# Forget-gate attention: one transpose for two heads, decay rows loaded beside the turned heads, six fillers at the opening

## The chip, the core and the metric

The kernel runs on one core of a Trainium2 chip. The metric is the device time of one execution in microseconds (us). The core has a matrix engine (TensorE, PE in the rows), VectorE (DVE), ScalarE (ACT), GpSimd (POOL) and SyncE (SP), each with its own instruction queue that is worked off in order; they wait for one another through semaphores. Matrix products are written to PSUM and have to be copied to SBUF by DVE or ACT. DMAs are issued from the queues of SP, ACT and POOL.

## What is computed

Two transformer blocks in float32, over 256 positions of width 1024, one after the other. The change touches the first attention of the first block, and in it the forget-gate heads ("fox"); around it stand gated feed-forward parts (ffn), a differential attention and, in the second block, two further mixers.

```python
def causal_block_attention(q, k, v, log_decay_cum=None):
    scale = q.shape[-1] ** -0.5
    for i in range(seq // Q_BLOCK):                     # blocks of 128 queries
        q0, q1 = i * Q_BLOCK, (i + 1) * Q_BLOCK
        s = einsum('bhqd,bhkd->bhqk', q[:, :, q0:q1], k[:, :, :q1]) * scale
        if log_decay_cum is not None:
            s = s + log_decay_cum[:, :, q0:q1, None] - log_decay_cum[:, :, None, :q1]
        ...                                             # causal mask, softmax, times v

def token_mixer(h, w_in, fox_forget_b, ...):
    fq, fk, fv, fgate, dq, dk, dv = split(h @ w_in)     # 8 fox heads of 64, 4 differential heads
    log_f = log_sigmoid(fgate + fox_forget_b)
    c = cumsum(log_f, axis=1)                           # one row of 256 sums for each fox head
    fox_o = causal_block_attention(fq, fk, fv, c)
    ...                                                 # differential attention, then @ w_out
```

The sums c enter the scores of a fox head as two further rows: the queries carry (c, 1) and the keys (1, -c) beside their 64 features, so one product of 66 rows gives q.k + c[t] - c[s].

## The kernel before

**Weights.** Every weight matrix comes in pieces of 128 x 2048. SP loads a piece into one of three slots (raw), ACT rounds it (hi, line 1207), DVE takes the rest (lo, line 1779), and PE multiplies the two parts in three products (lines 582, 585, 586). PE waits for a piece's lo. All engines' queues are written out by hand, step by step, so the order of the code is the order of the work.

**The projection (w_in).** Its blocks of 512 columns are copied out of PSUM by ACT for the first 128 positions and by DVE for the second (evac, line 1957 on DVE) into the large tile proj. Blocks 0 to 2 are the differential q, k, v, blocks 3 and 4 the fox q and k, block 5 the fox v. Half blocks are numbered h = 0 to 23; after each, ACT and DVE do the copy-out that is due and the next piece's hi or lo (after, next_lo). Meanwhile DVE works out log f (line 2243), clears qd_sb (line 2245, its tile is called att_dec in the rows), and PE forms the sums c with three small products (lines 1078 to 1080) behind h = 8. PE goes on to the attention when the decay columns are written (aug_ready).

**POOL's rotation.** When blocks 0 and 1 are copied out (evac_a and evac_d at 2), POOL rotates parts of the differential q and k, 12 operations (lines 1723 to 1728), and raises roped. PE waits for roped before it turns pair 0.

**The attention (diff_and_fox).** It goes by pairs p: 0 to 3 are the four differential heads, 4 to 7 the fox heads two by two. For each pair PE turns q and k by transposes (turn_qk, line 854) into the PSUM bank turned; ACT copies q out (q_out), DVE copies k out (k_out); PE forms scores (lines 872 to 877; the products with id16 and mask16 add the causal mask), DVE finds maxima, ACT takes exp, PE turns the weights (line 884) and multiplies with v (lines 896 to 898), DVE scales the result (line 2052 for fox heads). Products of projections that are still due (behind, products) stand between these steps. For the fox pairs each head's 64 columns and 2 decay columns lie together in proj (AUG = 66 columns a head), so a head is turned by itself: 8 transposes of 66 columns a pair, with both tiles of positions and q and k. The turned heads go to q_sb and k_sb (att_q and att_k in the rows), 66 rows each. The scores of pair 5 wait besides for DVE's scaling of two pieces of the turned differential output (fill_scaled, line 1797; turn_scaled).

**The opening.** Until the first weights are there, PE multiplies zeros (warm_up, line 646): 7 fillers, the first four transposes of x, 3 fillers, then the first product (line 667), which waits for ACT's first rounded part.

Of the kernel before, what the change touches and what calls it, by code (L numbers as in the profile page):

```python
# [11 lines left out]
ALU = mybir.AluOpType  # L12
# [27 lines left out]
FQ, FK, FV, DQ, DK, DV, MIX = 0, 8 * AUG, 16 * AUG, 16 * AUG + 512, 16 * AUG + 1024, 16 * AUG + 1536, 16 * AUG + 2048  # L40
# [80 lines left out]
def build(nc, x_d, wg_d, wu_d, wd_d, win_d, wout_d, win2_d, whg_d, wat_d, wout2_d,  # L121
          fixed_d, rows_d, post_d, rel_d, level_d, hot_d, out_d, row_d, skew_d):

    with ExitStack() as ctx:
# [80 lines left out]
        def heads(ap, n):  # L205
# [28 lines left out]
        log_f_ready, decay_sum, aug_ready, padded = (  # L234
            sem("log_f_ready"), sem("decay_sum"), sem("aug_ready"), sem("padded"))
# [103 lines left out]
        def win_place(b, t):  # L339

            if b < 3:
                return proj[:, t, DQ + b * BLK:DQ + (b + 1) * BLK]
            if b < 5:
                return heads(proj[:, t, (b - 3) * 8 * AUG:(b - 2) * 8 * AUG], 8)[:, :, 0:64]
            return proj[:, t, FV:FV + BLK]

# [232 lines left out]
        def _(pe):  # L579
# [68 lines left out]
            def first_block():  # L648
# [28 lines left out]
                warm_up(3)  # L677
# [165 lines left out]
            def turn_qk(p):  # L843

                kind, i = pair(p)
                for n in range(2):
                    for h in range(1 if kind == 1 else 2):
                        for t in range(TT):
                            if kind == 0:
                                src = proj[:, t, ((FQ, FK)[n] + (2 * i + h) * AUG):((FQ, FK)[n] + (2 * i + h + 1) * AUG)]  # L850
                            else:
                                col = (DQ, DK)[n] + i * P if kind == 1 else (AQ, AK)[n] + i * S + h * P
                                src = proj[:, t, col:col + P]
                            mm = pe.transpose(turned[0:src.shape[1], n, h * S + t * P:h * S + (t + 1) * P], src, idn)  # L854
                mm.then_inc(qkT_full, 1)

            def scores(p):
                kind = pair(p)[0]
                pe.wait_ge(qT_ready, p + 1)
                pe.wait_ge(kT_ready, p + 1)  # L860
                if p in (1, 2, 3, 9, 10, 11):
# [5 lines left out]
                rows_used = AUG if kind == 0 else P  # L867
                for h in range(2):
                    q = (qd_sb if kind == 1 else q_sb)[0:rows_used, h, :]
                    k = k_sb[0:rows_used, 0 if kind == 1 else h, :]  # L870
# [328 lines left out]
        def _(act):  # L1199
# [151 lines left out]
            def q_out(p):  # L1351
                kind = pair(p)[0]
# [1209 lines left out]
```

## Time and profile before

| | |
|---|---|
| time, median of 3 runs | 1019.68 us (1019.23 to 1020.27) |
| the profiled execution | 1020.19 us |
| its span, first to last instruction | 1018.4 us |
| PE busy | 1012.3 us, 99% |
| DVE busy | 713.0 us, 70% |
| ACT busy | 486.9 us, 48% |
| POOL busy | 201.5 us, 20% |
| TensorE's granted clock, mean of the span | 1.00 |

The time is what a run takes on the device; the span is what the profile sees, from the first to the last instruction. Busy times are shares of the span. PE's busy time counts pipelined matmuls whose ends are modelled, so a stretch of PE is best read by the starts of its instructions. A timeline row gives start, duration, engine, line, operation, what it writes and reads, how many instructions are merged, and in brackets the idle time before it with what ended it.

### The profile page before, as it was taken

How to read it: one execution, taken by the hardware profiler on the slowest of the kernel's cores; microseconds unless marked ns; L12 is line 12 of the kernel's file. 1: busy time of each engine (PE TensorE's matmuls, PEld its weight loads, DVE VectorE, ACT ScalarE, POOL GpSimd, SP SyncE). 2: the span in 40 equal slices, each digit the busy share in tenths (PEclk: the TensorE clock that was granted, in tenths of full speed). 3: DMA queues.
4: the chain of work that ended last, by engine and by line, in shares of the span. 5: the costliest groups of instructions: out<-in, count | busy, mean ns of one | idle time of the engine just before them, and what ended most of it. 6: DMA issues, size and time to landing. Idle time of an engine off the chain costs nothing.

```text
span 1018.4 us, 14449 instructions
## 1 busy us (share of the span) xinstructions
PE 1012.3 (99%) x5240; PEld 856.1 (84%) x5240; DVE 713.0 (70%) x821; ACT 486.9 (48%) x606; POOL 201.5 (20%) x198
## 2 busy tenths in 40 slices
PE   8999999999999999999999999999999999999998
PEld 6888888888888888888888888888888888888887
DVE  6766666765678767676764589986877677666664
ACT  6544344554555544444544454545446354434342
POOL 2313131121100223222110070033000002313130
PEclk9999999999999999999999999999999999999999
DMA  9664556664324556565746554444435645555551
GB/s 317 213 206 165 206 169 222 227 189 128 119 84 166 166 170 206 182 208 182 244 149 196 178 166 138 146 128 161 136 102 182 204 167 206 165 206 170 201 197 51
DMA packets 116809, 178.62 MB, mean 175 GB/s; under 512 B 5656, under 2 KB 73760, under 8 KB 116640
## 3 DMA queue, kind: packets, MB, share of 16 engines
q1 hardware_dynamic: 115952, 174.82, 51.4%
q0 software_dynamic: 512, 1.55, 0.6%
q10 hardware_dynamic: 304, 1.70, 0.5%
q8 instruction: 27, 0.44, 0.2%
q14 instruction: 14, 0.11, 0.0%
HBM read 176.98 MB, written 2.63 MB: 176 GB/s over the span
## 4 chain that ended last, share of the span: by engine, by line
PE 99%; DMA 0%; ACT 0%; issue 0%; SPq 0%; DVE 0%
PE acc L582 11%; PE acc L586 11%; PE acc L585 11%; PE tp L762 10%; PE gu L762 10%; PE gu L765 5%; PE tp L765 5%; PE tp L582 4%; PE tp L586 4%; PE tp L585 4%; PE gu L582 4%; PE gu L586 4%; PE gu L585 4%; PE acc L1002 2%; PE gu L872 1%; PE acc L854 1%
## 5 line engine op out<-in xcount | busy, mean ns | idle before, releaser
L1779 DVE TENSOR_TENSOR wlo<-raw,whi 128x2048 fp32r<-128x2048 f32 x149 | 349.1, 2346 | 157.2 <-ACT whi L1207 156.4
L1207 ACT ACTIVATE whi<-raw 128x2048 fp32r<-128x2048 f32 x150 | 285.8, 1908 | 61.8 <-PE acc L586 26.7
L762 PE MATMUL tp<-act_in,whi 128*128 128x512 f32 x432 | 103.0, 391 | 0.0
L762 PE MATMUL gu<-act_in,whi 128*128 128x512 f32 x432 | 102.6, 390 | 0.0
L1700 POOL TENSOR_TENSOR sil<-sil,tmp 128x256 f32<-128x256 f32 x54 | 88.9, 1646 | 33.6 <-ACT sil L1279 33.6
L1698 POOL TENSOR_TENSOR tmp<-tmp 128x256 f32<-128x256 f32 x54 | 39.8, 737 | 281.5 <-DVE tmp L1898 281.5
L762 PEld LDWEIGHTS gu<-act_in,whi 128*128 128x128 f32 x432 | 80.9, 188 | 16.6
L582 PE MATMUL acc<-whi,hT_hi 128*128 128x512 f32 x240 | 94.0, 392 | 0.0
L585 PE MATMUL acc<-wlo,hT_hi 128*128 128x512 f32 x240 | 93.7, 390 | 0.0
L586 PE MATMUL acc<-whi,hT_lo 128*128 128x512 f32 x240 | 93.4, 389 | 0.0
L762 PEld LDWEIGHTS tp<-act_in,whi 128*128 128x128 f32 x432 | 79.7, 188 | 16.1 <-issue 0.4
L1284 ACT ACTIVATE hT_hi<-hid 128x256 fp32r<-128x256 f32 x54 | 22.2, 417 | 138.5 <-DVE hid L1909 129.6
L582 PE MATMUL tp<-whi,act_in 128*128 128x512 f32 x192 | 77.4, 403 | 0.0
L586 PE MATMUL tp<-whi,act_in 128*128 128x512 f32 x192 | 75.0, 391 | 0.0
L585 PE MATMUL tp<-wlo,act_in 128*128 128x512 f32 x192 | 74.8, 390 | 0.0
L582 PE MATMUL acc<-whi,act_in 128*128 128x512 f32 x176 | 70.9, 403 | 0.0
L1279 ACT ACTIVATE sil<-tmp 128x256 f32<-128x256 f32 x54 | 22.1, 409 | 100.3 <-POOL tmp L1698 100.3
L586 PE MATMUL acc<-whi,act_in 128*128 128x512 f32 x176 | 68.7, 391 | 0.0
L585 PE MATMUL acc<-wlo,act_in 128*128 128x512 f32 x176 | 68.6, 390 | 0.0
L1681 POOL TENSOR_SCALAR ms<-sums 128x1 f32<-128x1 f32 (+2 forms) x20 | 11.3, 566 | 268.9 <-ACT junk L1229 159.7
L765 PEld LDWEIGHTS gu<-act_in,wlo 128*128 128x128 f32 x432 | 55.4, 191 | 2.1
L765 PEld LDWEIGHTS tp<-act_in,wlo 128*128 128x128 f32 x432 | 55.4, 191 | 2.1
(327 smaller groups left out, 1830.5 us busy)
## 6 DMA issues: line engine op xcount, KB each, us to landing
raw<-in_w_in SPq DMA_DIRECT2D x96, 512.0 KB, 4.5
raw<-in_down SPq DMA_DIRECT2D x66, 512.0 KB, 4.0
raw<-in_gate SPq DMA_DIRECT2D x64, 512.0 KB, 4.1
raw<-in_up SPq DMA_DIRECT2D x64, 512.0 KB, 4.7
raw<-in_w_out SPq DMA_DIRECT2D x16, 512.0 KB, 4.6
raw<-in_w_branch_hg SPq DMA_DIRECT2D x8, 512.0 KB, 4.6
raw<-in_w_branch_attn SPq DMA_DIRECT2D x8, 512.0 KB, 4.7
post<-in_post_gains SPq DMA_DIRECT2D x3, 512.0 KB, 6.7
```

What stands on the lines that cost most here:

```text
L582: pe.matmul(out, hi, w_hi, start=start, stop=False)
L585: pe.matmul(out, hi, w_lo, start=False, stop=False)
L586: return pe.matmul(out, lo, w_hi, start=False, stop=stop)
L762: pe.matmul(banks[:, a, :], w_hi[:, i, a * P:(a + 1) * P], both, start=i == 0, stop=False)
L765: mm = pe.matmul(banks[:, a, 0:S], w_lo[:, i, a * P:(a + 1) * P], act_in[:, i, 0, :], start=False, stop=i == KT - 1)
L1002: mm = pe.matmul(acc[:, hh, i // 2, i % 2 * 256:i % 2 * 256 + QN], k_at(t, h), hg_queries(t)[:, h, :], start=True, stop=True)
L1207: act.activation(split_weights(k)[0], raw[:, k % RING, :], ACT.Copy).then_inc(hi_ready, 1)
L1279: act.activation(sil[:, a, :], gate[:, a, :], ACT.Silu).then_inc(sil_ready, 1)
L1284: act.activation(hT_hi[:, a, :], hid[:, a, :], ACT.Copy).then_inc(hT_hi_ready, 1)
L1698: pool.tensor_tensor(gate[:, a, :], gate[:, a, :], row, ALU.mult).then_inc(gate_scaled, 1)
L1700: pool.tensor_tensor(sil[:, a, :], sil[:, a, :], row, ALU.mult).then_inc(sil_scaled, 1)
L1779: dve.tensor_tensor(w_lo, raw[:, k % RING, :], w_hi.bitcast(F32), ALU.subtract).then_inc(lo_ready, 1)
```

## The change

1. The fox q and k of all heads lie in proj without gaps (FQ, FK at multiples of 512), and two heads are turned by one transpose of 128 columns: 4 transposes a pair instead of 8.
2. The turned heads no longer go to q_sb and k_sb. Each head has a place of its own in a free part of proj (fox_q in the first tile of positions, fox_k in the second). Of a pair, the first head takes rows 0 to 63, the second rows 64 to 127, since that is where the transpose puts them. ACT and DVE so write two pieces of 64 x 256 where they wrote one of 66 x 512.
3. The decay rows lie beside them: rows 64 and 65 for a first head, rows 0 and 1 for a second, whose rows 2 to 63 are zero. The scores use 66 rows for a first head and 128 for a second. DVE clears and sets these rows with six memsets of 1024 elements in a partition, ahead of the memset of qd_sb.
4. The sums c are formed as rows (8 x 256 instead of 128 x 16), copied by DVE to a scratch tile, stored to DRAM by POOL, and loaded by POOL with four small DMAs. POOL does this behind its rotation and ahead of the norms of the differential heads. The scores of pair 4 wait for the loads (aug_in).
5. The opening has 6 fillers ahead of the first product instead of 3.

```diff
-FQ, FK, FV, DQ, DK, DV, MIX = 0, 8 * AUG, 16 * AUG, 16 * AUG + 512, 16 * AUG + 1024, 16 * AUG + 1536, 16 * AUG + 2048
+FQ, FK, FV, DQ, DK, DV, MIX = (512 * n for n in range(7))
+FOX_AT = 5120
...
+        fox_q, fox_k = (heads(proj[:, t, FOX_AT:FOX_AT + 8 * S], 8) for t in range(TT))
+        decay_rows = xs[0:8, 1, 0:S]
...
-                warm_up(3)
+                warm_up(6)
...
                 for n in range(2):
-                    for h in range(1 if kind == 1 else 2):
+                    for h in range(2 if kind == 2 else 1):
                         for t in range(TT):
-                            if kind == 0:
-                                src = proj[:, t, ((FQ, FK)[n] + (2 * i + h) * AUG):((FQ, FK)[n] + (2 * i + h + 1) * AUG)]
...
-                            mm = pe.transpose(turned[0:src.shape[1], n, h * S + t * P:h * S + (t + 1) * P], src, idn)
+                            col = ((FQ, FK)[n] + i * P, (DQ, DK)[n] + i * P, (AQ, AK)[n] + i * S + h * P)[kind]
+                            mm = pe.transpose(turned[:, n, h * S + t * P:h * S + (t + 1) * P], proj[:, t, col:col + P], idn)
...
+                if p == 4:
+                    pe.wait_ge(aug_in, 16 * 4)
...
-                rows_used = AUG if kind == 0 else P
                 for h in range(2):
+                    rows_used = AUG if kind == 0 and h == 0 else P
+                    if kind == 0:
+                        q, k = (a[0:rows_used, 2 * i + h, :] for a in (fox_q, fox_k))
...
-            pe.matmul(tp[:, 1, 0:8], tri, f[0], start=True, stop=True)
-            pe.matmul(tp[:, 1, 8:16], ones, f[0], start=True, stop=False)
-            pe.matmul(tp[:, 1, 8:16], tri, f[1], start=False, stop=True).then_inc(decay_sum, 1)
+            pe.matmul(tp[0:8, 1, 0:P], f[0], tri, start=True, stop=True)
+            pe.matmul(tp[0:8, 1, P:S], f[0], ones, start=True, stop=False)
+            pe.matmul(tp[0:8, 1, P:S], f[1], tri, start=False, stop=True).then_inc(decay_sum, 1)
...
+                elif kind == 0:
+                    act.activation(fox_q[0:64, 2 * i, :], turned[0:64, 0, 0:S], ACT.Copy, scale=FOX_SCALE)
+                    act.activation(fox_q[64:P, 2 * i + 1, :], turned[64:P, 0, 0:S], ACT.Copy, scale=FOX_SCALE)\
+                       .then_inc(qT_ready, 1)
...
             pool.nop().then_inc(roped, 1)
+            pool.wait_ge(aug_ready, 1)
+            pool.wait_ge(rows_spread, 16)
+            pool.dma_start(bass.AP(tensor=row_d.tensor, offset=0, ap=[[S, 8], [1, S]]), decay_rows).then_inc(aug_out, 16)
+            pool.wait_ge(aug_out, 16)
+            for a, r in ((fox_q, 0), (fox_k, 1)):
+                for h, at in ((0, 64), (1, 0)):
+                    dst = a.rearrange("p (i two) n -> p i two n", two=2)[at + r:at + r + 1, :, h, :]
+                    pool.dma_start(dst, bass.AP(tensor=row_d.tensor, offset=h * S, ap=[[8 * S, 1], [2 * S, 4], [1, S]]))                        .then_inc(aug_in, 16)
             norm("diff")
...
-                    dve.tensor_copy(k_sb[0:AUG, :, :], heads(turned[0:AUG, 1, :], 2)).then_inc(kT_ready, 1)
+                    dve.tensor_copy(fox_k[0:64, 2 * i, :], turned[0:64, 1, 0:S])
+                    dve.tensor_copy(fox_k[64:P, 2 * i + 1, :], turned[64:P, 1, 0:S]).then_inc(kT_ready, 1)
...
+            for a, one in ((fox_q, -1.0), (fox_k, 1.0)):
+                of_pairs = a.rearrange("p (i two) n -> p i two n", two=2)
+                link(dve.memset(of_pairs[0:64, :, 1, :], 0.0))
+                dve.memset(of_pairs[0:2, :, 1, :], one)
+                dve.memset(of_pairs[64:66, :, 0, :], one)
             dve.memset(qd_sb, 0.0).then_inc(padded, 1)
...
-                    dve.wait_ge(evac_a, 2)
-                    c = tp[:, 1, 0:16].rearrange("p (t h) -> p t h", t=TT)
...
-                    dve.tensor_scalar(q2[:, :, :, 64], c, 8.0, None, ALU.mult)
-                    dve.tensor_scalar(k2[:, :, :, 65], c, -1.0, None, ALU.mult)
-                    dve.memset(q2[:, :, :, 65], 8.0)
-                    dve.memset(k2[:, :, :, 64], 1.0).then_inc(aug_ready, 1)
+                    dve.tensor_copy(decay_rows, tp[0:8, 1, 0:S]).then_inc(aug_ready, 1)
```

On DVE, from the log of the gates (lf) to the decay columns, this stood in a row before (att_dec is qd_sb, wlo the rest of a weight piece, proj<-acc a copy-out of the projection):

```order
L2243 SCALAR_TENSOR_TENSOR lf<-lf 128x16
L2245 MEMSET att_dec 128x512
L1779 TENSOR_TENSOR wlo<-raw,whi 128x2048
L1957 TENSOR_SCALAR proj<-acc,rstd 128x512
L1779 TENSOR_TENSOR wlo<-raw,whi 128x2048 x2
L2255 TENSOR_SCALAR proj<-tp 128x2x8
L2256 TENSOR_SCALAR proj<-tp 128x2x8
L2257 MEMSET proj 128x2x8
L2258 MEMSET proj 128x2x8
```

and this stands there now:

```order
L2259 SCALAR_TENSOR_TENSOR lf<-lf 128x16
L2263 MEMSET proj 64x4x256
L2264 MEMSET proj 2x4x256
L2265 MEMSET proj 2x4x256
L2263 MEMSET proj 64x4x256
L2264 MEMSET proj 2x4x256
L2265 MEMSET proj 2x4x256
L2266 MEMSET att_dec 128x512
L1794 TENSOR_TENSOR wlo<-raw,whi 128x2048
L1972 TENSOR_SCALAR proj<-acc,rstd 128x512
L1794 TENSOR_TENSOR wlo<-raw,whi 128x2048 x2
L2273 COPY xs<-tp 8x256
```

Six memsets have come in ahead of the first weight rest and of the copy-out of block 1, which POOL's rotation waits for; the four small operations behind the rests have become one copy.

On POOL, from the end of the rotation to the first norm of the differential heads, this stands now (before, the last line of the rotation was followed by the norm at once):

```order
L1732 TENSOR_TENSOR xs<-proj,fixed 128x128
L1733 TENSOR_TENSOR xs<-proj,fixed 128x128
L1734 TENSOR_TENSOR proj<-xs 128x16x8
L1735 TENSOR_TENSOR proj<-xs 128x16x8
L1739 DMA bias_rows<-xs 8x256
L1744 DMA proj<-bias_rows 1x4x256 x4
L1688 TENSOR_SCALAR ms<-sums 128x2
```

The five DMAs stand between the rotation and the norm.

On PE, the scores of pair 4 and the turn of pair 5 behind them, before (id and mask add the causal mask):

```order
L872 MATMUL tp<-att_k,att_q 128x256
L874 MATMUL tp<-mask,id 128x128
L875 MATMUL tp<-att_k,att_q 128x128
L877 MATMUL tp<-mask,id 128x128
L872 MATMUL tp<-att_k,att_q 128x256
L874 MATMUL tp<-mask,id 128x128
L875 MATMUL tp<-att_k,att_q 128x128
L877 MATMUL tp<-mask,id 128x128
L854 MATMUL acc<-fixed,proj 66x128 x8
```

and now:

```order
L876 MATMUL tp<-proj 128x256
L878 MATMUL tp<-mask,id 128x128
L879 MATMUL tp<-proj 128x128
L881 MATMUL tp<-mask,id 128x128
L876 MATMUL tp<-proj 128x256
L878 MATMUL tp<-mask,id 128x128
L879 MATMUL tp<-proj 128x128
L881 MATMUL tp<-mask,id 128x128
L854 MATMUL acc<-fixed,proj 128x128 x4
```

The order is the same; the turn has 4 transposes for 8, and the scores read the heads' own places.

## Rows read from the trace of the kernel before

**Rows 1.** The page, part 1: busy us (share of the span) xinstructions of each engine.

```profile
PE 1012.3 (99%) x5240; PEld 856.1 (84%) x5240; DVE 713.0 (70%) x821; ACT 486.9 (48%) x606; POOL 201.5 (20%) x198
```

**Rows 2.** The page, part 4: the chain that ended last, by engine.

```profile
PE 99%; DMA 0%; ACT 0%; issue 0%; SPq 0%; DVE 0%
```

**Rows 3.** Timeline of PE, opening: start us, us, engine line op out<-in xcount [idle before <-releaser].

```profile
5.03 0.81 PE L646 MATMUL gu<-junk 128*128 128x512 bf16 x3
...
7.35 0.47 PE L667 MATMUL gu<-whi,act_in 128*128 128x512 f32 x1 [1.51 <-ACT whi L1469]
```

**Rows 4.** Stretches of PE, opening: stretch, us, PE busy (x), granted clock, DMA, GB/s.

```profile
6.00:7.00 1.00, 0.00 (x0) 1.00 1.07 372
```

**Rows 5.** Timeline of DVE, projection, 217 to 231 us.

```profile
217.34 0.48 DVE L2245 MEMSET att_dec<- 128x512 f32 x1
220.43 2.29 DVE L1779 TENSOR_TENSOR wlo<-raw,whi 128x2048 fp32r<-128x2048 f32 x1 [2.61 <-ACT whi L1207]
222.64 0.74 DVE L1957 TENSOR_SCALAR proj<-acc,rstd 128x512 f32<-128x512 f32 x1
223.30 2.28 DVE L1779 TENSOR_TENSOR wlo<-raw,whi 128x2048 fp32r<-128x2048 f32 x1
228.15 2.55 DVE L1779 TENSOR_TENSOR wlo<-raw,whi 128x2048 fp32r<-128x2048 f32 x1 [2.56 <-ACT whi L1207]
```

**Rows 6.** Groups by form, DVE: line, operation, shapes, xcount | busy us, mean ns | idle.

```profile
L1982 DVE COPY att_k<-acc 66x512 f32<-66x512 f32 x4 | 2.7, 685 | 2.4 <-PE acc L854 2.4
L1980 DVE COPY att_k<-acc 128x256 f32<-128x256 f32 x4 | 1.7, 425 | 6.0 <-PE acc L854 6.0
...
L2258 DVE MEMSET proj<- 128x16 f32 x1 | 0.1, 72 | 0.0
```

**Rows 7.** Timeline of PE, projection: decay products, piece 5's first product, pair 0's turn.

```profile
222.52 0.28 PE L1078 MATMUL tp<-lf,fixed 128*128 128x8 f32 x2
...
223.11 0.48 PE L582 MATMUL acc<-whi,act_in 128*128 128x512 f32 x1
...
225.94 0.39 PE L582 MATMUL acc<-whi,act_in 128*128 128x512 f32 x1
...
234.10 0.60 PE L854 MATMUL acc<-fixed,proj 128*128 128x128 f32 x4
```

**Rows 8.** Timeline of POOL: the rotation's blocked operations, its last, the first norm.

```profile
223.56 2.33 POOL L1723 TENSOR_TENSOR xs<-proj,fixed 128x128 f32<-128x128 f32 x1 [17.83 <-DVE proj L1957]
...
228.51 2.48 POOL L1724 TENSOR_TENSOR xs<-proj,fixed 128x128 f32<-128x128 f32 x1
...
232.29 0.46 POOL L1728 TENSOR_TENSOR proj<-xs 128x128 f32<-128x128 f32 x1
256.39 0.19 POOL L1681 TENSOR_SCALAR ms<-sums 128x2 f32<-128x2 f32 x1 [23.64 <-ACT junk L1393]
```

**Rows 9.** Groups by form, PE: scores of 128 and of 66 rows, 128 columns.

```profile
L875 PE MATMUL gu<-att_k,att_dec 128*128 128x128 f32 x16 | 3.5, 302 | 0.0
...
L875 PE MATMUL gu<-att_k,att_q 66*128 66x128 f32 x8 | 1.7, 301 | 0.0
```

**Rows 10.** DMA issues: out<-in queue op xcount, KB each, median us to landing.

```profile
rel<-in_rel_table POOLq DMA_DIRECT2D x1, 1.0 KB, 4.6
```

**Rows 11.** Timeline of PE, attention: turns of pairs 2 and 4 and what follows.

```profile
253.84 0.60 PE L854 MATMUL acc<-fixed,proj 128*128 128x128 f32 x4
254.27 0.39 PE L896 MATMUL gu<-proj,att_pT 128*128 128x128 f32 x2
...
275.19 1.03 PE L854 MATMUL acc<-fixed,proj 128*66 128x128 f32 x8
276.06 0.39 PE L896 MATMUL gu<-proj,att_pT 128*128 128x128 f32 x2
```

**Rows 12.** Timeline of PE, attention: the first product of pair 5's scores.

```profile
286.43 0.67 PE L872 MATMUL gu<-att_k,att_q 66*128 66x256 f32 x2
```

**Rows 13.** Timeline of DVE, attention: the scaling that pair 5's scores wait for.

```profile
285.01 1.28 DVE L1797 TENSOR_TENSOR tmp<-gu,fixed 128x512 f32<-128x512 f32 x2
```

More of the change, by code:

```diff
@@ L233, in build @@
         gate_product, gate_abs, gate_log = sem("gate_product"), sem("gate_abs"), sem("gate_log")
-        log_f_ready, decay_sum, aug_ready, padded = (
-            sem("log_f_ready"), sem("decay_sum"), sem("aug_ready"), sem("padded"))
+        log_f_ready, decay_sum, aug_ready, aug_out, aug_in, padded = (
+            sem("log_f_ready"), sem("decay_sum"), sem("aug_ready"), sem("aug_out"), sem("aug_in"), sem("padded"))
         lb_in, lb_exp, lam_in, lam_exp = sem("lb_in"), sem("lb_exp"), sem("lam_in"), sem("lam_exp")
@@ L343, in win_place @@
             if b < 5:
-                return heads(proj[:, t, (b - 3) * 8 * AUG:(b - 2) * 8 * AUG], 8)[:, :, 0:64]
+                return proj[:, t, (b - 3) * BLK:(b - 2) * BLK]
             return proj[:, t, FV:FV + BLK]
+        fox_q, fox_k = (heads(proj[:, t, FOX_AT:FOX_AT + 8 * S], 8) for t in range(TT))
+        decay_rows = xs[0:8, 1, 0:S]
         def fill_bank(u, i):
@@ L846, in turn_qk @@
                 for n in range(2):
[L847 removed]
+                    for h in range(2 if kind == 2 else 1):
                         for t in range(TT):
[L849 to L854 removed]
+                            col = ((FQ, FK)[n] + i * P, (DQ, DK)[n] + i * P, (AQ, AK)[n] + i * S + h * P)[kind]
+                            mm = pe.transpose(turned[:, n, h * S + t * P:h * S + (t + 1) * P], proj[:, t, col:col + P], idn)
                 mm.then_inc(qkT_full, 1)
             def scores(p):
[L858 removed]
+                kind, i = pair(p)
                 pe.wait_ge(qT_ready, p + 1)
                 pe.wait_ge(kT_ready, p + 1)
+                if p == 4:
+                    pe.wait_ge(aug_in, 16 * 4)
                 if p in (1, 2, 3, 9, 10, 11):
@@ L866, in scores @@
                     pe.wait_ge(turn_scaled, scaled_n(turn_n(T_WOUT) + 1))
-                rows_used = AUG if kind == 0 else P
                 for h in range(2):
-                    q = (qd_sb if kind == 1 else q_sb)[0:rows_used, h, :]
-                    k = k_sb[0:rows_used, 0 if kind == 1 else h, :]
+                    rows_used = AUG if kind == 0 and h == 0 else P
+                    if kind == 0:
+                        q, k = (a[0:rows_used, 2 * i + h, :] for a in (fox_q, fox_k))
+                    else:
+                        q, k = (qd_sb if kind == 1 else q_sb)[:, h, :], k_sb[:, 0 if kind == 1 else h, :]
                     lt, el = late(p)[:, h * S:(h + 1) * S], early(p)[:, h * P:(h + 1) * P]
@@ L1351, in q_out @@
             def q_out(p):
-                kind = pair(p)[0]
+                kind, i = pair(p)
                 act.wait_ge(qkT_full, p + 1)
@@ L1357, in q_out @@
                     act.activation(qd_sb[64:P, 1, :], turned[64:P, 0, 0:S], ACT.Copy, scale=FOX_SCALE).then_inc(qT_ready, 1)
-                else:
-                    r = AUG if kind == 0 else P
-                    act.activation(q_sb[0:r, :, :], heads(turned[0:r, 0, :], 2), ACT.Copy,
-                                   scale=FOX_SCALE if kind == 0 else cols[:, G_QG:G_QG + 1]).then_inc(qT_ready, 1)
+                elif kind == 0:
+                    act.activation(fox_q[0:64, 2 * i, :], turned[0:64, 0, 0:S], ACT.Copy, scale=FOX_SCALE)
+                    act.activation(fox_q[64:P, 2 * i + 1, :], turned[64:P, 0, 0:S], ACT.Copy, scale=FOX_SCALE)\
+                       .then_inc(qT_ready, 1)
+                else:
+                    act.activation(q_sb[:, :, :], heads(turned[:, 0, :], 2), ACT.Copy,
+                                   scale=cols[:, G_QG:G_QG + 1]).then_inc(qT_ready, 1)
             def exps(p):
@@ L1976, in k_out @@
             def k_out(p):
-                kind = pair(p)[0]
+                kind, i = pair(p)
                 dve.wait_ge(qkT_full, p + 1)
```

1 line of the change is left out of this document (removed).

## The prediction

> **What bounds the kernel now.** I read the busy times first [rows 1]: TensorE (PE) is busy 1012.3 of 1018.4 us, so only some 6 us of the span are not matmul. The chain of waits says the same [rows 2]: 99% of the chain that ended last is PE. So an edit counts only if it takes time out of PE's own row, or makes PE wait where it does not wait now. DVE, ACT, POOL and the DMAs matter only at the points where PE waits for them, and each has to be looked at in its own place. I then went through the timelines in three places: the opening, the stretch from 217 to 235 us in which the first projection ends and the attention begins, and the attention of pairs 4 to 7 (the forget-gate pairs) from 275 us on.
>
> **The opening: three more fillers, nothing.** The three fillers ahead of the first product take 0.81 us together, and PE then stands for 1.51 us until ACT has split the first weights [rows 3]. Three more, at the same 0.27 us, end at about 6.65 us; the first product starts at 7.35 us. That idle time hides them, with 0.7 us over; if it were gone they would cost at most 0.8 us. Can they gain? Only if the idle time cost PE its clock. The granted clock is 1.00, its upper level of 2.4 GHz, in the very microsecond in which PE does nothing [rows 4], so there is nothing to win back. I take 0, with ends of -0.3 and +0.8 us.
>
> **The projection stage: six memsets on DVE.** They stand right behind the log of the gates, ahead of the memset of qd_sb (before: at 217.34 us). Each writes 1024 elements in a partition. The trace has no memset that long; it has 512 elements at 0.48 us [rows 5] and 16 at 72 ns [rows 6], a slope of 0.83 ns an element, so 0.91 us for 1024, and with the small overlap of neighbours about 0.87 us from start to start. Two of them are followed by a wait of DVE for itself; I allow 0.1 us each, small beside the bounds. Sum: 6 x 0.87 + 0.2 = 5.4 us. The other bound is the rate of DVE's copies, 425 ns for 256 and 685 ns for 512 elements [rows 6], 1.02 ns an element: 1.2 us for 1024, 7.0 us in all. The lower bound is what the short memsets give if two partitions cost less than 128, which no row shows. I take 5.4, since that is the slope of the same operation.
> By the Trainium skill, "VectorE: DVE Perf Modes", section "Zero memsets can be issued as uint32 (trn2)", a memset takes one cycle an element; with the 0.96 GHz of its page "Trainium Kernel Development and Optimization", section "NeuronCore Architecture", that is an estimate of 1.07 us each and 6.6 us in all, so 1.2 us more wait at the end of the sum below; the trace's 512 elements in 0.48 us are less than the 0.53 us that this gives, so I stay with the row.
>
> Behind the memsets DVE's queue holds: the rest of a weight piece (lo of piece 5 of w_in), the copy-out of block 1, the rests of pieces 6 and 7, then the decay. Before, DVE had 2.61 us of idle time ahead of the first of these, which started at 220.43 us [rows 5]. Now the memsets end at 217.34 + 5.4 = 222.75, qd_sb at 223.2, and piece 5 starts 2.8 us late, at 223.2, and ends at 225.5. PE takes piece 5 at 225.94 us [rows 7]. So this wait stays covered, by 0.4 us. The copy-out, before at 222.64, comes at 225.4 and ends at 226.2; piece 6 runs from 226.1 to 228.4, piece 7 from 228.3 to 230.9.
>
> **The same delay on POOL, and there it is not covered.** POOL's rotation (12 operations, lines 1723 to 1728) waits for that copy-out. Before, it began at 223.56 and ended at 232.29 + 0.46 = 232.75 [rows 8], and PE, which waits for it before it turns pair 0, came to that turn at 234.10 [rows 7]: 1.35 us of cover, less about 0.2 us for the signal (0.14 us at the place in rows 12 and 13, and a nop ahead of it). Two of the twelve operations took 2.33 and 2.48 us where the others take 0.44: each began while DVE ran a weight rest, and ended 0.3 us after it (225.89 against 225.58, 230.99 against 230.70) [rows 5, 8]. So a rest on DVE holds POOL up for its whole length. Now POOL begins at 226.35. Its first operation ends 0.3 us after piece 6, at 228.7; the second is held by piece 7 and ends at 231.2; the other ten at 0.44 us (the last four before took 1.76 us) end at 235.65. With 0.2 us for the signal PE turns pair 0 at 235.85 instead of 234.10: **+1.75 us**. PE has nothing to put there, since its queue is in order, and everything behind shifts by as much. If the first operation too is held until piece 7 is done, the end is 235.8; the bounds come from the memsets: 7.0 instead of 5.4 us puts it to +3.35 us.
>
> **The decay itself.** The three products become 128 columns wide with 8 columns of weights; each is two records. Before they took 222.52 to 223.11, 0.59 us [rows 7]. The nearest rows with 128 columns show a busy share of 3.5/16 = 0.22 us a record [rows 9], so at most 1.3 us; the lower bound is the 0.59 us of now. Since the turn of pair 0 now starts when POOL is done, up to 1.5 us more ahead of it costs nothing; without that wait I would add 0.1 to 0.7 us. DVE's four small operations become one copy of 256 elements (0.4 us); PE's wait for it (aug_ready) comes at about 231.4, and DVE is there at 231.3; a miss of a few tenths would hide in the same wait.
>
> **The rows by way of DRAM.** POOL issues one store, waits for it, then four loads. All of it stands behind the rotation and ahead of the norms of the differential heads. POOL's small loads land after 4.6 us [rows 10]. Even at 2 us for each issue, more than I expect, the store is in by 242.3, the loads are issued by 250.3 and in by 255. The first norm is wanted at 256.39, after POOL has stood for 23.64 us [rows 8], and it needs only the issues. The new wait for the rows stands before the scores of pair 4, at 278.8 us (now 1.75 later): cover of some 25 us. Cost 0. Queues SP and ACT are not touched.
>
> **Pairs 4 to 7: the turns.** Four transposes of 128 columns take 253.84 to 254.27 = 0.43 us; eight of 66 take 275.19 to 276.06 = 0.87 us [rows 11]. A transpose costs PE the same at 66 or 128 columns, so half as many save 0.44 us a pair, 1.76 us in four. The scores are not dearer: the 66-row and the 128-row form take 301 and 302 ns [rows 9]. On ACT and DVE one copy of 66 x 512 becomes two of 64 x 256: DVE 685 ns becomes about 0.76 us [rows 6], 0.08 us more, where the next step waits for DVE.
> Not all four pairs can keep it. Pair 4: PE goes on into products that are ready; 0.44 saved. Pair 5: after its turn PE comes to the scores of pair 5, which start at 286.43 [rows 12], 0.14 us after DVE has scaled two pieces of the output turn (285.01 + 1.28 = 286.29) [rows 13]. DVE's queue up to there starts from the scores of pair 4, ahead of the turn, so it gets no earlier; the 0.44 us turn into a wait, and DVE's 0.08 us come on top: -0.08 saved. Pairs 6 and 7: DVE's queue starts from the turn itself, so it moves with it; 0.44 less up to 0.08, 0.40 each. Sum: 0.44 - 0.08 + 0.40 + 0.40 = **1.16 us saved**. Ends: 1.76 (no wait takes it) and 0.36 (only pair 4 keeps it, pair 5 as above).
>
> **The sum.** +1.75 - 1.16 + 0 = +0.6 us. The profiled execution took 1020.19 us, of which 1018.4 are span and 1.8 lie around it; it would take 1020.8. The median of the runs shown is 0.5 us lower, 1019.68: I forecast **1020.3 us**. A measurement of this kernel can tell about 0.2%, 2.04 us, from no change; so this is no change.
>
> **Rivals.**
> *The rotation is not late* (the memsets are short, or the first rests leave POOL room). It decides from a delay of 1.05 us of DVE, that is memsets of 3.7 us in all, 0.57 us each. Against it: the slope of the memset rows. For it: four of the six write two partitions only. Then the turns' 1.16 us stay, less 0.1 to 0.7 for the decay: 1018.7 us, and 1017.9 if all four pairs keep theirs. Chance 0.18.
> *The memsets run at the rate of copies*, the slow side, at the one place PE meets POOL's rotation: +3.35 - 1.16 = +2.2, 1021.9 us. Slower by more than 0.2% from memsets of 1.15 us on. On its way piece 5 is late for PE too (226.7 and later against 225.94), which does not add, since PE's later wait takes it in. For it: the copies' slope, and the longest memset seen is half as long. Against: the two memset rows. Chance 0.15.
> *The turns save nothing*, each pair ending in a wait as pair 5 does: +1.75 + 0.3 = +2.1, 1021.8 us. For it: what the rows show at pair 5. Against: pairs 4, 6 and 7 have their DVE work behind the turn. Chance 0.05.
> Anything else, such as the loads landing late: 0.04.
>
> **Chances and range.** The forecast (1019.7 to 1020.9) has 0.58. Faster by over 0.2% (under 1017.64) takes the low end of the first rival and something unseen: 0.06. Slower (over 1021.72): half of the second and third and the tail, 0.16. Within: 0.78. The range, 1018.3 to 1022.0, takes in most of both first rivals and leaves out under 2 in 10.
>
> **What would show it.** Each memset at 0.9 us, and piece 5's rest starting near 223.2 us; POOL's rotation ending near 235.7; PE standing 1.5 to 1.8 us before the turn of pair 0, with POOL named; four transposes in 0.43 us at pairs 4 to 7, and a wait of some 0.5 us before the scores of pair 5, for DVE; the loads landed by 255 us; the first product at 7.35 us as now. I am wrong if PE does not stand before the turn of pair 0, if the scores of pair 4 wait for a DMA, or if the opening moves.

## The result, and the profile after

| | before | after |
|---|---|---|
| median of the runs made together (11 each) | 1019.53 us | 1022.13 us (1021.74 to 1022.32) |
| the profiled execution | 1020.19 us | 1021.74 us |
| its span | 1018.4 us | 1019.9 us |

The ratio is 1.0024, with a 95% interval of 1.0015 to 1.0034. The kernel became slower by 2.6 us. That is just past the 0.2% (2.04 us) which the prediction set as its bound, and the interval reaches to both sides of that bound. The forecast, 1020.3 us, is 1.8 us too low, and 1022.13 lies 0.13 us above the upper end of the range.

The page of after, parts 1 and 4 (busy us, share of the span and instructions of each engine; the chain of waits by engine), answers to [rows 1, 2]:

```profile
PE 1012.3 (99%) x5227; PEld 854.0 (84%) x5227; DVE 718.6 (70%) x828; ACT 487.4 (48%) x610; POOL 203.9 (20%) x203
...
PE 96%; DVE 2%; POOL 1%; issue 1%; ACT 0%; POOLq 0%
```

PE is busy for as long as before, 1012.3 us, and the span is 1.5 us longer. So the loss is waiting, and the chain now has shares of DVE and POOL that it did not have. The waits of PE between 195 and 330 us of after (engine, line, what it waited for: us in total, times, longest) name the places; the kernel before shows none there:

```profile
PE acc L854 <- POOLq L1736: 1.4, 1, 1.4
PE acc L586 <- DVE wlo L1794: 0.7, 1, 0.7
PE gu L876 <- DVE tmp L1812: 0.5, 1, 0.5
PE tp L876 <- DVE proj L2068: 0.3, 1, 0.3
```

The first two are the delay of DVE at piece 5 and of POOL at the turn of pair 0; the last two stand before the scores of pairs 5 and 6. The timeline of DVE in after, projection (start us, us, engine line operation; in brackets the idle time before and what ended it), answers to [rows 5]:

```profile
216.51 0.91 DVE L2263 MEMSET proj<- 64x1024 f32 x1 [0.15 <-issue]
217.69 0.91 DVE L2264 MEMSET proj<- 2x1024 f32 x1 [0.27 <-DVE proj L2263]
218.85 0.91 DVE L2265 MEMSET proj<- 2x1024 f32 x1 [0.25 <-issue]
220.01 0.91 DVE L2263 MEMSET proj<- 64x1024 f32 x1 [0.25 <-issue]
221.19 0.91 DVE L2264 MEMSET proj<- 2x1024 f32 x1 [0.27 <-DVE proj L2263]
222.35 0.91 DVE L2265 MEMSET proj<- 2x1024 f32 x1 [0.25 <-issue]
223.42 0.48 DVE L2266 MEMSET att_dec<- 128x512 f32 x1 [0.15 <-issue]
223.82 2.23 DVE L1794 TENSOR_TENSOR wlo<-raw,whi 128x2048 fp32r<-128x2048 f32 x1
225.97 0.74 DVE L1972 TENSOR_SCALAR proj<-acc,rstd 128x512 f32<-128x512 f32 x1
```

Each memset's record is 0.91 us long, as forecast, but the next one starts 1.16 to 1.18 us after it (the memset of qd_sb 1.07 us after the last), also where nothing but the engine's own queue lies between ("issue"). From the first memset to that of qd_sb (att_dec in the rows) it is 6.91 us, not 5.4. POOL's rotation in after, its two blocked operations, its last, the store and the four loads, and the first norm, answers to [rows 8]:

```profile
226.87 2.32 POOL L1730 TENSOR_TENSOR xs<-proj,fixed 128x128 f32<-128x128 f32 x1 [22.07 <-DVE proj L1972]
229.16 2.48 POOL L1731 TENSOR_TENSOR xs<-proj,fixed 128x128 f32<-128x128 f32 x1
...
235.57 0.45 POOL L1735 TENSOR_TENSOR proj<-xs 128x128 f32<-128x128 f32 x1
236.68 0.62 POOL L1739 DMA_DIRECT2D bias_rows<-xs  x1 [0.66 <-POOL proj L1735]
238.67 1.99 POOL L1744 DMA_DIRECT2D proj<-bias_rows  x4 [1.37 <-DMA bias_rows<-xs]
258.54 0.18 POOL L1688 TENSOR_SCALAR ms<-sums 128x2 f32<-128x2 f32 x1 [17.88 <-ACT junk L1400]
```

And PE in after: the decay's first product, piece 5's first product, the turn of pair 0 [rows 7], the turn of pair 4 and what follows [rows 11], the scores of pair 5 [rows 12] and of pair 6:

```profile
221.68 0.39 PE L1082 MATMUL tp<-fixed,lf 128*8 128x128 f32 x2
...
226.10 0.50 PE L586 MATMUL acc<-whi,act_in 128*128 128x512 f32 x1 [0.65 <-DVE wlo L1794]
...
236.22 0.63 PE L854 MATMUL acc<-fixed,proj 128*128 128x128 f32 x4 [1.43 <-POOLq L1736]
...
277.31 0.60 PE L854 MATMUL acc<-fixed,proj 128*128 128x128 f32 x4
277.75 0.39 PE L900 MATMUL gu<-proj,att_pT 128*128 128x128 f32 x2
...
288.55 0.67 PE L876 MATMUL gu<-proj 66*128 66x256 f32 x2 [0.45 <-DVE tmp L1812]
...
295.64 0.67 PE L876 MATMUL tp<-proj 66*128 66x256 f32 x2 [0.33 <-DVE proj L2068]
```

**The account by stages**, from the starts of PE's rows in one profile of each kernel (us; "turn 0" is the turn of pair 0, "fills" the first transposes behind the attention, line 625 before and 629 after). The last three columns are experiments of the next section ("both" is the memsets on POOL with all of DVE's new order).

| from, to | before | after | memsets on POOL | DVE's order alone | both |
|---|---|---|---|---|---|
| start, first product | 7.35 | 6.43 | 6.70 | 6.63 | 6.37 |
| decay, turn 0 | 11.58 | 14.54 | 11.77 | 11.57 | 11.77 |
| turn 0, scores 4 | 44.68 | 44.26 | 44.27 | 44.68 | 44.24 |
| scores 4, scores 5 | 7.65 | 8.07 | 8.07 | 7.58 | 7.15 |
| scores 5, scores 6 | 7.21 | 7.09 | 7.09 | 6.92 | 6.61 |
| scores 6, scores 7 | 7.00 | 6.59 | 6.59 | 6.93 | 6.56 |
| scores 7, fills | 10.51 | 10.51 | 10.50 | 10.52 | 10.50 |

After loses 2.96 us at the turn of pair 0 and gains 0.53 in the forget-gate pairs: +2.4, close to the 2.6 of the medians. The two executions that were profiled differ by only 1.55 us since the first product came 0.92 us earlier in that of after; that start differs from execution to execution (below).

### The profile page after: what moved, and what is told of

Its sections match the earlier page's. It is cut to its first block, busy times and chain, and to the rows that moved or that the text cites. A ratio compares the mean times of both kernels' runs of the same rounds, so it can differ in the third digit from the quotient of the medians.

```text
span 1019.9 us, 14439 instructions
## 1 busy us (share of the span) xinstructions
PE 1012.3 (99%) x5227; PEld 854.0 (84%) x5227; DVE 718.6 (70%) x828; ACT 487.4 (48%) x610; POOL 203.9 (20%) x203
## 3 DMA queue, kind: packets, MB, share of 16 engines
q0 software_dynamic: 672, 1.57, 0.6%
## 4 chain that ended last, share of the span: by engine, by line
PE 96%; DVE 2%; POOL 1%; issue 1%; ACT 0%; POOLq 0%
PE acc L586 10%; PE acc L589 10%; PE acc L590 10%; PE tp L766 10%; PE gu L766 10%; PE gu L769 5%; PE tp L769 5%; PE tp L586 4%; PE tp L590 4%; PE tp L589 4%; PE gu L586 4%; PE gu L590 4%; PE gu L589 4%; PE acc L1006 2%; PE gu L876 1%; PE acc L888 1%
```

## The experiments

All were timed against the kernel before on the same chip; its medians there were 1019.35 us (for the first four), 1019.32 (the next three) and 1019.41 us (the last two). Where two kernels were not timed side by side, I compare their distances from the kernel before.

**The memsets alone.** The kernel before, with the six memsets on columns of proj that nothing reads:

```diff
+            fox_q, fox_k = (heads(proj[:, t, 5120:5120 + 8 * S], 8) for t in range(TT))
+            for a, one in ((fox_q, -1.0), (fox_k, 1.0)):
+                of_pairs = a.rearrange("p (i two) n -> p i two n", two=2)
+                link(dve.memset(of_pairs[0:64, :, 1, :], 0.0))
+                dve.memset(of_pairs[0:2, :, 1, :], one)
+                dve.memset(of_pairs[64:66, :, 0, :], one)
```

> The kernel before with the six memsets alone, in the place they have in the changed kernel, on columns of proj that nothing reads; nothing else of the change. Theory (DVE's queue delays the copy-out, that delays POOL's rotation, PE waits for it): 2.9 us slower than before, 1022.4, with PE standing some 0.7 us at piece 5 and some 1.4 to 2.2 us before the turn of pair 0, POOL named. Rival (the time comes from the loads by way of DRAM, the wider scores or the fillers, all missing here): within 0.5 us of before.

Measured: 1022.44 us, ratio 1.0029 (1.0018 to 1.0041). PE waits 1.6 us for POOL before the turn of pair 0 and 0.9 us at piece 5, its only waits between 195 and 330 us:

```profile
PE acc L854 <- POOLq L1729: 1.6, 1, 1.6
PE acc L582 <- DVE wlo L1779: 0.9, 1, 0.9
```

Decay to turn 0 takes 14.64 us. So the whole loss, and the place of it, is there without any other part of the change.

**The memsets on POOL.** The changed kernel, with the six memsets moved out of DVE's queue to POOL's, ahead of the rotation, where POOL stands idle for 22 us (17.83 us in the kernel before [rows 8]); they start behind a wait for PE:

```diff
+            pool.wait_ge(piece_used, N_WIN + 2)
...
+                link(pool.memset(of_pairs[0:64, :, 1, :], 0.0))
...
-                link(dve.memset(of_pairs[0:64, :, 1, :], 0.0))
```

> The changed kernel with the six memsets on POOL, ahead of its rotation, where it stood idle for 17.8 us before; nothing else differs. Theory: the wait before the turn of pair 0 and the wait for piece 5 go, 2.96 us less than the changed kernel less what the wider decay costs then; what is left is the gain of the turns, 0.5 us, so 1019.0 to 1019.3, 0.2 to 0.5 us under before. Rival (the loads or the turns cost the time): still 1021.5 or more.

Measured: 1019.38 us, ratio 0.9999 (0.9990 to 1.0008). Its waits of PE between 195 and 330 us are these two:

```profile
PE gu L876 <- DVE tmp L1818: 0.4, 1, 0.4
PE tp L876 <- DVE proj L2074: 0.3, 1, 0.3
```

Both waits of the projection are gone, and with them 2.6 us: this kernel lies 0.03 us above the kernel before, the changed one 2.60. What is left in the account by stages is the price of the other parts: decay to turn 0 is 0.19 us longer than before, 0.16 of it from the decay's first product to the product behind the three (0.75 us for 0.59), and the forget-gate pairs save 0.53. A net gain of 0.3 us is less than the interval can tell from nothing.

**The memsets in two groups.** The three of the queries where they are, the three of the keys behind the copy-out of block 1 and the lo of piece 5:

```diff
+            def rows_set(a, one):
...
+            rows_set(fox_q, -1.0)
+            block_out(N_WIN, 0, 7)
+            next_lo(N_WIN, 0, 5)
+            rows_set(fox_k, 1.0)
...
```

> The changed kernel with all six memsets on DVE, but the copy-out of block 1 and the rest of piece 5 moved between the first three and the last three. No work is removed, only the order on DVE differs. Theory (what counts is what the copy-out stands behind): POOL's rotation begins near 220.5 us and is done before PE comes to pair 0, so 1019.0 to 1019.5 as with the memsets on POOL. Rival (DVE simply has too much work in this stage, or memsets themselves hold POOL up): 1021 us or more, the wait only moved to another piece.

Measured: 1020.69 us, ratio 1.0012 (1.0003 to 1.0021): half of the loss is left, which I had not expected. PE's wait in the projection (first fence), DVE's timeline and PE's there:

```profile
PE acc L586 <- DVE xs L2282: 0.9, 1, 0.9
```

```profile
226.49 0.48 DVE L2272 MEMSET att_dec<- 128x512 f32 x1 [0.15 <-issue]
226.90 4.67 DVE L1794 TENSOR_TENSOR wlo<-raw,whi 128x2048 fp32r<-128x2048 f32 x2
231.49 0.41 DVE L2282 COPY xs<-tp 8x256 f32<-8x256 f32 x1
```

```profile
231.95 0.50 PE L586 MATMUL acc<-whi,act_in 128*128 128x512 f32 x1 [0.85 <-DVE xs L2282]
```

POOL's rotation began at 220.91 and ended in time (232.30; turn 0 at 234.81 with no wait before it). But the second group now pushes the rests of pieces 6 and 7, and with them the copy of the decay, for which PE waits (aug_ready): 0.85 us. I had looked only at the two waits that the change had made, and not at the third thing in DVE's queue.

**Three fillers in the opening.** The changed kernel with warm_up(3) in the place of warm_up(6):

> The changed kernel with 3 fillers ahead of the first product instead of 6. Theory (the fillers lie in PE's idle time): as the changed kernel, 1022.1, within 0.3 us. Rival 1 (six fillers end after the weights' first part is there and push the first product back): 0.3 to 0.6 us faster. Rival 2 (the fillers keep the clock or win time): 0.3 us or more slower.

Measured: 1022.08 us, against 1022.13 with six. In the profiles the first product starts at 7.35, 7.30, 7.05, 6.70 and 6.63 us where there are three fillers (6.49 in the last run below) and at 6.70, 6.61, 6.43, 6.37 and 6.36 where there are six, so a later start went more often with three; the medians show nothing of it. What it goes by is ACT: in all eleven profiles the first product starts 0.14 or 0.15 us after ACT's first rounded part is done, which is at 7.21 us in the kernel before, at 6.29 in the changed one, and at 6.34 in the last run, with three fillers.

**How long a memset is.** The kernel before with runs of memsets of one size each on columns that nothing reads (an entry of runs is the tile of positions, the first partition, the first column and the length; the four of 512 begin at partition 0):

```diff
...
+            runs += [(0, 64, 5120, 1024), (0, 64, 6144, 1024), (0, 0, 5120, 2048)]
+            for n, (t, p, col, wide) in enumerate(runs):
+                ins = dve.memset(proj[p:p + 64, t, col:col + wide], 0.0)
...
```

> The kernel before, with runs of VectorE's memsets on columns that nothing reads: eight of 64 elements, four of 128, four of 256, four of 512, two of 1024 and one of 2048, contiguous, on 64 partitions. In the changed kernel a memset of 1024 elements shows 0.91 us, and the next one starts 1.17 us after it. Theory A (the engine writes one element in 1.04 ns, and the record leaves a part out): start to start 2.2 us at 2048, 1.17 at 1024, 0.64 at 512, 0.37 at 256, 0.24 at 128, 0.17 at 64. Theory B (the rate is that of the record, 0.83 ns an element, and a fixed gap of 0.25 us stands behind each): 0.73 at 512, 0.52 at 256, 0.41 at 128, 0.37 at 64. Theory C (the gap belongs to the rows taken by pairs of heads, with strides): a contiguous 1024 shows 0.9 to 1.0. The time is only the price of about 11 us of memsets and tells nothing.

The groups of DVE by form (line, operation, shape, count | busy us, mean ns | idle), and below them the starts of the four of 512 and of the longer ones in the timeline:

```profile
L2254 DVE MEMSET proj<- 64x512 f32 x4 | 1.9, 485 | 0.3
...
L2254 DVE MEMSET proj<- 64x64 f32 x8 | 0.7, 112 | 0.1
```

```profile
219.25 0.48 DVE L2254 MEMSET proj<- 64x512 f32 x1
219.80 0.48 DVE L2254 MEMSET proj<- 64x512 f32 x1
220.34 0.48 DVE L2254 MEMSET proj<- 64x512 f32 x1
220.88 0.48 DVE L2254 MEMSET proj<- 64x512 f32 x1
```

```profile
221.61 0.91 DVE L2254 MEMSET proj<- 64x1024 f32 x1 [0.25 <-issue]
222.69 0.91 DVE L2254 MEMSET proj<- 64x1024 f32 x1 [0.16 <-issue]
224.06 1.76 DVE L2254 MEMSET proj<- 64x2048 f32 x1 [0.46 <-issue]
225.88 0.48 DVE L2257 MEMSET att_dec<- 128x512 f32 x1
```

The records grow by 0.83 ns an element, just as the two rows of before said. The starts do not: 0.54 us apart at 512, 1.08 at 1024, and 4.27 us for the 4096 elements from 221.61 to 225.88, which is 1.04 ns an element. Theory B, a fixed gap of 0.25 us, would have 0.73 at 512 and falls; the gap grows with the size (0.06 at 512, 0.16 at 1024). The rate of theory A holds; its own numbers do not, since they keep a further 0.1 us for each memset (0.64 at 512, 1.17 at 1024). The Trainium skill states this rate ("VectorE: DVE Perf Modes", section "Zero memsets can be issued as uint32 (trn2)"): one cycle an element, which with the 0.96 GHz of the Trainium skill's page "Trainium Kernel Development and Optimization", section "NeuronCore Architecture", is an estimate of 1.04 ns. Where a record and the rate differ, the time is missing ahead of the record: the idle time before the 2048 is 0.46 us, before a 1024 behind a 1024 it is 0.16.

Theory C, that the rest of 0.09 us (1.16 to 1.18 in the change, 1.08 here) belongs to the strides, is not shown. The first contiguous 1024 here has 0.25 us of idle time ahead of it, as much as the strided ones of the change, and the contiguous memset of qd_sb has 0.15 in the changed kernel and 0.06 here. What fits these rows, where the strides do not, is the place: the first 1024 here, and the memset of qd_sb in the changed kernel, begin at another partition than the memset before them, those with 0.16 and 0.06 at the same one. Of the five memsets behind the first in the change, three begin at another partition and two wait for the signal of the linked one before them; no run tests the place by itself.

The time of this kernel, 1025.79 us in one run, is not the price of its memsets alone. PE stands for 3.11 us at piece 5, waiting for DVE, and the granted clock, 1.00 up to 227.5 us, is 0.50 (the level of 1.2 GHz) from 228 to 234 us and 1.00 again from 235 us on; part of the 6.5 us over the kernel before is this.

**DVE's order in the attention.** With the memsets on POOL, the norm of head 3 and the lo of half 19 ahead of the maxima of pair 4 and the copies of pair 5:

```diff
+                next_lo(N_WIN, 0, 19)
+                normed(3)
                 maxima(4)
                 k_out(5)
-                normed(3)
-                next_lo(N_WIN, 0, 19)
```

> The changed kernel with the six memsets on GpSimd, and in VectorE's row of the attention the norm of head 3 and the lo of half 19 put ahead of the maxima of pair 4 and the copies of pair 5 (before: behind them). With the memsets on GpSimd alone it took 1019.38 us, TensorE waited 0.43 us ahead of the scores of pair 5 for VectorE's scaled tile, and the stretch from the scores of pair 4 to those of pair 5 was longer by that much than in the kernel before. Theory (the two copies of 0.86 us, which stand ahead of the scaled tiles in VectorE's row, make that wait, and the row has room ahead of them): the wait goes, 1019.38 - 0.43 = 1018.9 us. Rival (VectorE is the bound over the whole stretch, so that the wait only moves to the next place at which TensorE reads from it): 1019.4 us, and the wait stands ahead of the softmax or of the turn of pair 5 instead.

Measured: 1018.33 us, ratio 0.9991 (0.9982 to 1.0000), 1.0 us less than with the memsets on POOL alone (0.99 us under the kernel before instead of 0.03 above it), where I had expected 0.43. The wait before the scores of pair 5 is gone and stands nowhere else. It was worth more than its record: in the kernel with the memsets on POOL, PE's timeline has one more late start ahead of it, of which the list of waits says nothing:

```profile
281.76 0.39 PE L589 MATMUL acc<-wlo,act_in 128*128 128x512 f32 x1
281.99 0.39 PE L590 MATMUL acc<-whi,act_in 128*128 128x512 f32 x1
282.45 1.09 PE L629 MATMUL gu<-fixed,proj 128*128 128x128 f32 x8
```

The two products follow one another at 0.23 us; to the transposes it is 0.46. The transposes of line 629 read the normed head 3, which stood behind the two copies in DVE's queue. In the new order they start 0.23 us after the product before them. The list understates the other wait too: it counts from the end of a product's record, 0.39 us after its start, where the next instruction would have started after 0.23, so 0.16 us are left out. Together 0.43 + 0.16 + 0.23 = 0.82 of the 0.92 us by which the stretch from the scores of pair 4 to those of pair 5 became shorter (8.07, now 7.15).

**And the second fill behind the output of pair 4.** In addition:

```diff
-                fill_rest(T_WOUT, 1)
                 output(4)
+                fill_rest(T_WOUT, 1)
```

> As the run with the norm and the lo moved earlier, and the rest of the second fill put behind the output of pair 4 (before: ahead of it). With the memsets on GpSimd alone TensorE waited 0.33 us ahead of the scores of pair 6 for VectorE's output of pair 4. Theory: that wait goes too, 1018.9 - 0.3 = 1018.6 us, faster than the kernel before by 0.8. Rival (the product that needs the second fill becomes late by the 0.85 us of the output, or the wait stands elsewhere): 1018.9 to 1019.4 us.

Measured: 1017.70 us, ratio 0.9985 (0.9976 to 0.9994); the list of PE's waits between 195 and 330 us is empty again. It is 0.63 us less than the run before it, where I had expected 0.3. This kernel beats both, by 1.6 us the one before and by 4.2 us the changed one.

**That order alone.** The kernel before with both moves in DVE's queue and nothing else:

> The kernel before, with VectorE's row of the attention in the order of the fastest kernel so far (1017.70 us against 1019.32 for the kernel before on the same chip): norm of head 3 and lo of half 19 ahead of the maxima of pair 4, rest of the second fill behind the output of pair 4. Theory (TensorE waits nowhere in these pairs in the kernel before but for 0.07 us ahead of the scores of pair 5, so the new order alone is worth at most that, and the 1.6 us come from the four turns of 0.36 us in the place of 0.79): 1019.2 to 1019.4 us. Rival (the order alone gives the gain, the turns little): 1017.8 to 1018.5 us.

Measured: 1018.84 us, ratio 0.9995 (0.9986 to 1.0004): not told from no change. Its median is 0.57 us below, between the two expectations: 0.36 us under the theory's lower end and 0.34 over the rival's upper end. So the order alone may be a third of the 1.6 us. In the account by stages the order takes 0.07 + 0.29 + 0.07 us from pairs 5 to 7: the kernel before had a late start at pair 6 too, though its list of waits is empty. A sign of it is in the first product's record, 0.67 us where PE had stood, 0.60 where it had not:

```profile
293.64 0.67 PE L872 MATMUL tp<-att_k,att_q 66*128 66x256 f32 x2
```

```profile
292.58 0.60 PE L872 MATMUL tp<-att_k,att_q 66*128 66x256 f32 x2
```

The first line is of before, the second of this kernel. With the order in both, the turns are worth 76.63 - 75.06 = 1.57 us from turn 0 to the fills (the last two columns of the table), 0.39 a pair.

**Three fillers again**, in the fastest kernel:

> The fastest kernel so far (memsets on GpSimd, VectorE's new order) with three fillers in the opening in the place of six. In the changed kernel three and six fillers came out alike (1022.08 and 1022.13 us). Theory (the first product waits for its weights either way): 1017.7 us, within 0.3. Rival (the three fillers more bring the first product 0.6 us forward, as the profiles of single runs show: 7.0 to 7.4 us with three, 6.4 to 6.7 with six): 1018.3 us.

Measured: 1017.55 us, with six 1017.70; the first product starts at 6.49 us in its profile. Twice no difference between three and six that could be told: the start of the first product moves with ACT's first rounded part, not with the fillers.

## Why the prediction was right or wrong, step by step

- **What bounds the kernel: right.** PE's busy time did not change; every loss is a wait or a late start of PE at a place that can be named.
- **The opening, 0: right** by the medians of two pairs of kernels. The trace of one execution would have shown a gain of 0.9 us, which the kernels with three fillers show as well (6.49 and 6.63 us). The prediction named a moved opening as a sign that it is wrong; the opening did move in that trace, from 7.35 to 6.43 us, with ACT's first rounded part (7.21 and 6.29 us).
- **The six memsets, 5.4 us: wrong, and this is the step that failed.** They take 6.9. I had the length of the records right to the hundredth and took it for the time that the queue needs. The overlap of neighbours that I took off (0.87 for 0.91) goes the other way for memsets: the next one starts later than the record ends. The longer of the two rows on which I rested the slope, 512 elements at 0.48 us, stood alone, with nothing behind it to show a distance. The prediction had the better number beside it, 6.6 us by the Trainium skill's one cycle an element, and put it aside because a record of 0.48 us was shorter than the 0.53 that it gives; the starts of a run of them say 0.54. A rate of copies (7.0 us; six times its 1.2 is 7.2) was the other end that I kept, and it is where the kernel is: the copies' 1.02 ns an element are close to the 1.04 from start to start of the memsets.
- **Piece 5 covered by 0.4 us: wrong, by the same term.** With 1.5 us more of memsets PE stands 0.65 us there. As the rival said, this does not add, since the wait behind takes it in.
- **POOL's rotation late, and PE with it: right in mechanism**, with 2.96 us in the place of 1.75. The two operations held by DVE's rests, the other ten at 0.44 us, the signal of 0.2 us (rotation ended at 236.02, PE began at 236.22) came as described; from the first product on, the rotation ends 229.59 us later instead of 225.40, which is 4.19 us; less the cover of 1.15 that is 3.04, of which 0.08 lie ahead of the decay. The run with the memsets alone shows it by itself. The Trainium skill ("SBUF — State Buffer", section "Who interferes with whom") says that a VectorE instruction with two inputs in SBUF contends with a GpSimd instruction that reads from SBUF, that the ports they share are an exclusive lock, and that the order of issue decides which of the two is blocked. The trace agrees: 2.32 and 2.48 us for the two operations that began under a rest, 0.42 to 0.47 for the other ten.
- **The decay: right.** Hidden in the wait; without it (the memsets on POOL), 0.19 us, inside the 0.1 to 0.7.
- **The rows by way of DRAM, 0: right.** The loads are issued by 240.7, and one lands 3.5 us (the median of the four) after its issue; the scores of pair 4 begin at 280.48, with nothing between them and the product before. The first norm found POOL idle for 17.88 us.
- **The turns, -1.16: half right.** Four transposes take 0.44 us, as said, and pairs 4 and 7 save 0.42 and 0.41. The two copies are the term that was mis-sized: DVE's timelines of before (first group) and after (second group) at pair 5 show it:

```profile
281.82 0.68 DVE L1982 COPY att_k<-acc 66x512 f32<-66x512 f32 x1
282.42 0.47 DVE L2062 TENSOR_SCALAR proj<-proj,rstd 128x128 f32<-128x128 f32 x2
```

```profile
283.51 0.41 DVE L1997 COPY proj<-acc 64x256 f32<-64x256 f32 x1
283.94 0.43 DVE L1998 COPY proj<-acc 64x256 f32<-64x256 f32 x1
284.39 0.48 DVE L2078 TENSOR_SCALAR proj<-proj,rstd 128x128 f32<-128x128 f32 x2
```

 From the copy to the next operation it is 0.60 us before and 0.88 after: +0.28, not +0.08. For the one I had the record, 0.685, of which the next operation hides a part; the short ones hide nothing. At pair 5 that, and 0.12 us more behind the lo, make DVE's way from the scores of pair 4 to the scaled tiles 0.41 us longer (7.51 before, 7.92 after) and the stretch 0.42 longer, where I had 0.08. At pair 6 it takes 0.28 of the 0.44, and 0.12 is saved instead of 0.40. Together -0.53. The upper end of 1.76, "no wait takes it", was nearly there once DVE's order was changed (1.57).
- **The rivals.** The second, memsets at the rate of copies, is what happened: it had 1021.9 us and a chance of 0.15, its delay at the one place, and piece 5 late on the way. The first needed memsets of 0.57 us and was out. The third, the turns save nothing, is half true, since two of the four pairs end in a wait. The two mis-sized terms lie on the same side: 2.96 - 1.75 = 1.21 us at the turn of pair 0 and 1.16 - 0.53 = 0.63 at the turns of the forget-gate pairs are 1.84 us, and the forecast is 1.83 too low. That these agree to the hundredth is luck: the change was forecast as +0.6 and measured as +2.6, which is 2.0 apart, and the median that the forecast was added to, 1019.68, lies 0.15 above the one measured beside the change.
- **What was to be seen.** The memsets' 0.9 us came true and deceived; the right thing to ask for was the start of piece 5's rest, which came 1.45 us later behind the first memset (7.31 us) than forecast (5.86).

What stays open: why a memset's record leaves out a part that grows with its length, and what the further 0.12 us behind the lo at pair 5 are, and whether the 0.09 us of a memset in the change beyond 1.08 come from the strides or from the partition it begins at. The fillers' effect is below what these runs can tell.

## What to carry to other kernels

Price an instruction on a busy queue by the distance to the start of the next one behind it, never by its record; where the trace has no two in a row, the longer of the candidate prices belongs in the forecast, and not just in the range. Before a setup step is put on an engine, look which engine stands idle at that time: the same six memsets cost 2.6 us on DVE and nothing that could be measured on POOL, which stood idle for 17.8 us there in the kernel before. When a step on TensorE is made shorter, follow the queue of the engine that feeds its next step; here two thirds of the gain (1.57 us against 0.53) came only after DVE's work had been put in another order.

## What the runs showed of the hardware

- A memset on DVE holds the queue for 1.04 ns an element (4096 elements in 4.27 us) and, as the change has it, 1.13 to 1.15 (1024 elements in four runs of 256, each memset beginning at another partition or behind a signal), while its record shows 0.83. Two partitions cost as much as 64 (both 0.91 us, 1.16 to 1.18 from start to start).
- On POOL the same memset of 1024 elements has a record of 0.95 us and one follows the other at 1.00 us, also linked:

```profile
206.25 0.95 POOL L1725 MEMSET proj<- 64x1024 f32 x1 [1.16 <-PE gu L590]
207.26 0.95 POOL L1726 MEMSET proj<- 2x1024 f32 x1
```

- A wait of PE costs more than its idle time in the list: the 0.43 and 0.33 us before the scores of pairs 5 and 6 were worth 0.92 and 0.47 us between the starts of the scores, and 1.0 and 0.63 of the medians. Of each, 0.16 us is the end of the product's record (0.39 us) beyond the start that the next instruction would have had (0.23 us); of the 0.92, a further 0.23 is the late start of the transposes. Such late starts of about 0.2 us are in no list of waits; they are seen only in the distance of PE's starts.
